# A hybrid SSD and gMLP step on one core: the opening's first weight tile reads the rows without the adaLN shift

## The chip, the cores and the metric

One core of one Trainium2 chip runs the whole kernel. The metric is the device time of one execution in microseconds (us), lower being better. The kernel before took a median of 1444.05 us over three runs, 1443.5 to 1444.36.

## The reference, cut to what matters

Two layers work on 640 rows of 1024 channels: 128 context rows (v = 0) and 512 latent rows (v = 1), each kind with its own conditioning vector `c`. What the change touches is the head of a layer:

```
mod = silu(c) @ w_ada + b_ada ; shift, scale, gate = split(mod, 3)
h = rms_norm(x, norm_w) * (1 + scale) + shift
proj = h @ w_in          # xbc, z, dt, u, v, z_g, gl_m, gl_g
```

`xbc` goes on into a depthwise convolution and a scan, `dt` into the decays of the scan, and the rest into two branches that are merged, projected and added to `x`. After two layers there is a final norm. Since the projection is linear, (s + shift) @ w = s @ w + shift @ w, where s is the scaled row without the shift; the second term is one column for the context rows and one for the latent rows.

## The kernel before, in words

Everything is kept transposed: channels on the 128 partitions, in eight chunks k = 0 to 7, and the 640 rows along the free axis. The weights come as tiles of 1024 by 128, numbered t; a layer has 88. For each tile SP loads half a megabyte into a slot of `w_st` (two slots), POOL splits it into a rounded high part `w_hi` and a rest `w_lo` in four quarters (lines 509 to 515), and PE multiplies it with the rows, which are split the same way. One chunk (line 600) is six matmuls of 320 columns: high weight with high row, low weight with high row, high weight with low row, two halves each. There are two accumulators, `acc[0]` and `acc[1]`.

The order of each engine's work is written out by hand, and semaphores tie the engines together. The opening of layer 0 is what this text is about:

- SP loads the conditioning vectors, the rows `xr`, small vectors, and then sixteen half-megabyte pieces of `w_ada`: four jobs of four pieces. A job (L, q, h) gives half h (channel chunks 0 to 3 or 4 to 7) of the scale (q = 1) or the shift (q = 0). The order before is scale half 0, shift half 0, scale half 1, shift half 1, by `JOBS_FIRST`. The narrow `dt` weight and tile 0 come after the eighth piece, tile 1 and six constants last.
- One job on PE is `first_mm` (line 670, two halves that each need two pieces), a `row_copy` on ACT (line 1026), `first_tp` on PE (line 681), and `job_out` on DVE (lines 1407 and 1412), which makes `mods` and, for a scale, the multiplier `amul`. `job_read` counts jobs that are out.
- `before(k)` on DVE (line 1473) makes `h_pre`, the row scaled but not shifted. `h_high(k)` on ACT (line 1045) adds the shift and rounds into `h_hi`. `h_low(k)` on DVE (line 1467) makes the rest `h_lo`, which lies in the place of `h_pre`.
- `dt` has a product of its own: DVE scales its narrow weight (`dt_scaled`, line 1452), PE multiplies the plain rows with it (`dt_part`, line 614) and adds the shift's part as two columns (`dt_shift`, line 622).
- `keep_pace` (line 656) are matmuls whose result nobody reads.
- `opening` runs chunks 0 to 3 of tile 0, with jobs 2 and 3 between and behind them, then `dt`, then chunks 4 to 7. After it, tile 1 and all others follow. POOL begins to split tile 2 when tile 0 is done (`tile_done`), and ACT moves tile 0's accumulator into `raw` (line 1180), from which DVE runs the convolution (lines 1618 and 1620).

Of the kernel before, what the change touches and what calls it, by code (L numbers as in the profile page):

```python
# [124 lines left out]
JOBS_FIRST = [(0, q, h) for h in (0, 1) for q in (1, 0)]  # L125
# [54 lines left out]
def build(nc, xT, wts, wada, cT, bada, normw, finalw, ssmw, convw, dtb, alog, dskip, lnw, lnb,  # L180
# [114 lines left out]
    bst = new("bst", [P, NCH, 12])  # L295
# [52 lines left out]
    dtrow_ready, raw_ready = sem("dtrow_ready"), sem("raw_ready")  # L348
    sel_ready, v_made = sem("sel_ready"), sem("v_made")
# [55 lines left out]
    def _(sp):  # L405
# [33 lines left out]
        for n in range(4 * NF):  # L439
            L, q, hf = JOBS_FIRST[n // 4]  # L440
            sp.dma_start(ada_first(n), wada[L, q, hf, n % 4, :, :, :]).then_inc(pre_in[n // 2], 16)
            if n == 7:
                dt_weight(0)
                weight(0, 0)
        weight(1, 1)
        load_consts()
# [36 lines left out]
    def _(pool):  # L483
# [32 lines left out]

        base = own.n
        for slot in range(2):
            split(slot, 16, None)
# [16 lines left out]
    def _(pe):  # L536
# [89 lines left out]
        def opening(hi, lo):  # L626

            ready = (hhi_ready, h_ready, 0)
            for k in range(KC // 2):
                chunk(0, k, hi, lo, ready)  # L630
                if k == 1:
                    first_mm(2)
            first_tp(2)
            first_mm(3)
            first_tp(3)
            dt_part(0, 1)
            pe.wait_ge(job_read, NF)
            dt_shift(0)
            for k in range(KC // 2, KC):
                last = chunk(0, k, hi, lo, ready)  # L640
            last.then_inc(tile_done, 1)
# [242 lines left out]
        first_mm(1, range(DTG))  # L884
        first_tp(0)
        keep_pace(2)
        first_mm(1, range(DTG, KC))
        keep_pace(2)
        first_tp(1)
        dt_part(0, 0)  # L890
        for L in range(DEPTH):
# [17 lines left out]
            if L == 0:  # L909
                opening(*h)  # L910
# [7 lines left out]
            for p in range(1, T_G):  # L918
# [5 lines left out]
                if p in V_AT:  # L924
                    v_tile(T0 + p, V_AT.index(p) % 2, hooks=hooks,
                           ready=(hhi_ready, h_ready, L) if L > 0 and p < RAWT + 2 else None)
                else:
# [30 lines left out]
    def _(act):  # L958
# [77 lines left out]
        row_copy(1)  # L1036

        for L in range(DEPTH):
# [23 lines left out]
            if L == 0:  # L1062
                act.wait_ge(job_read, 2)
                for k in range(KC // 2):
                    h_high(k)
                act.wait_ge(norm_in, 48)
                A(ea[:, :], ea[:, :], ACT.Exp).then_inc(ea_ready, 1)
                row_copy(2)
                row_copy(3)
                act.wait_ge(job_read, NF)  # L1070
                for k in range(KC // 2, KC):
                    h_high(k)
# [4 lines left out]
                free(("dt", 0), A(halves(c_buf[0]), a[:, :, 0:HALF], ACT.Copy))  # L1077
                evacuated(act, ("dt", 0))
# [71 lines left out]
            for p in range(T_UZ):  # L1150
# [28 lines left out]
                for dst, src in pieces(acc_of(t), *raw_row(i), L):  # L1179
                    last = A(dst, src, ACT.Copy)  # L1180
# [180 lines left out]
    def _(dve):  # L1361
# [93 lines left out]
        for L in range(DEPTH):  # L1455
# [39 lines left out]
            if L == 0:  # L1495
                dve.wait_ge(rbc_ready, 1)
                for half in range(2):
                    k0 = KC // 2 * half
                    if half == 1:
                        dve.wait_ge(ea_ready, 1)  # L1500
                        for d in range(DEPTH):
                            last = TS(ea_diag[:, d, :], ident[0:32, 0:32], ea[:, d:d + 1], None, ALU.mult)
                        last.then_inc(diag_ready, 1)
                        job_out(2)
                    before(k0)
                    before(k0 + 1)
                    dt_scaled(0, k0, k0 + KC // 2)
                    before(k0 + 2)
                    job_out(2 * half + 1)
                    before(k0 + 3)  # L1510
                    for k in range(k0, k0 + KC // 2):
                        h_low(k)
# [507 lines left out]
```

## Time and profile before

| what | us |
|---|---|
| median of three runs | 1444.05 |
| the profiled execution's own time | 1443.57 |
| its span | 1441.8 |
| PE busy | 1425.8 (99% of the span) |
| POOL busy | 1023.6 (71%) |
| DVE busy | 975.0 (68%) |
| ACT busy | 474.2 (33%) |

The profiled execution lies 0.48 us below the median and has 1.8 us around its span. Starts in the timelines are counted from the span's start. A timeline line merges instructions that follow each other: its second number runs from the first one's start to the last one's end, and the x number is their count. Matmuls overlap, so the pace of a group is read from the start of one line to the start of the next. "PEclk" is the granted clock of TensorE: 1.00 is 2.4 GHz and 0.50 is 1.2 GHz.

### The profile page before, as it was taken

The page shows a single profiled execution, that of the slowest core. Times are in us where ns is not written, and L with a number is a line of the kernel's source. Part 1 is how long each engine was busy: PE and PEld are TensorE (multiplying, and loading weights), DVE is VectorE, ACT ScalarE, POOL GpSimd, SP SyncE. Part 2 cuts the span into 40 slices and gives each one's busy share as a digit, 9 for nine tenths or more (in the row PEclk, how much of TensorE's full clock was granted, in tenths as well). Part 3 has the DMA queues.
Part 4 walks back from the last instruction along what each step waited for, and adds up shares of the span by engine and source line. Part 5 has one row for each costly group of instructions (what it writes and reads, how often), then busy time and mean ns, then how long its engine had stood idle before and what let it go on. Part 6 is the DMA issues. An engine that isn't in the chain of part 4 may idle for free.

```text
span 1441.8 us, 27057 instructions
## 1 busy us (share of the span) xinstructions
PE 1425.8 (99%) x10191; PEld 1388.0 (96%) x10191; DVE 975.0 (68%) x1454; ACT 474.2 (33%) x1086; POOL 1023.6 (71%) x1421
## 2 busy tenths in 40 slices
PE   8999999999999999999999999999999999999997
PEld 5999998999999999999999999989999999999997
DVE  5865576674767678988879676567566876867234
ACT  4331223313766333001243323241257661320122
POOL 2688875596555589998859897658765556979772
PEclk9999999999999999999999999999999999999999
DMA  9112333113565565444332232421346565453222
GB/s 358 60 64 78 129 106 121 63 62 116 152 193 183 158 253 194 152 151 138 115 132 74 78 122 93 134 63 59 103 127 181 170 189 186 161 187 118 74 74 88
DMA packets 113838, 189.54 MB, mean 131 GB/s; under 512 B 12736, under 2 KB 76352, under 8 KB 112320
## 3 DMA queue, kind: packets, MB, share of 16 engines
q1 hardware_dynamic: 42736, 138.34, 29.1%
q10 hardware_dynamic: 70992, 49.63, 11.5%
q8 instruction: 81, 1.33, 0.4%
q14 instruction: 29, 0.24, 0.0%
HBM read 169.79 MB, written 18.15 MB: 130 GB/s over the span
## 4 chain that ended last, share of the span: by engine, by line
PE 96%; DVE 2%; DMA 1%; SPq 0%; ACT 0%; issue 0%; DVEq 0%; ACTq 0%
PE acc L600 78%; PE acc L567 6%; PE X L840 2%; PE X L805 2%; PE X L567 1%; PE X L825 1%; PE X L872 1%; DMA ada_pre<-in_wada 1%; PE X L851 1%; PE X L759 1%; DVE cv L1620 1%; PE X L649 0%; PE acc L718 0%; DVE h_pre L1473 0%; DVE xr L1936 0%; PE X L812 0%
## 5 line engine op out<-in xcount | busy, mean ns | idle before, releaser
L510 POOL CAST w_hi<-w_st 128x256 fp32r<-128x256 f32 x704 | 419.8, 610 | 396.1 <-issue 182.6
L514 POOL TENSOR_TENSOR w_lo<-w_st,w_hi 128x256 fp32r<-128x256 f32 x704 | 641.5, 921 | 0.0
L600 PE MATMUL acc<-h_hi,w_hi 128*128 128x320 f32 x1744 | 406.3, 314 | 0.7 <-ACT h_hi L1045 0.7
L600 PE MATMUL acc<-h_lo,w_hi 128*128 128x320 f32 x1744 | 397.8, 309 | 1.1 <-DVE h_lo L1467 1.1
L600 PE MATMUL acc<-h_hi,w_lo 128*128 128x320 f32 x1744 | 397.2, 309 | 0.0
L600 PEld LDWEIGHTS acc<-h_hi,w_hi 128*128 128x128 f32 x1744 | 288.6, 188 | 10.5 <-issue 7.8
L600 PEld LDWEIGHTS acc<-h_lo,w_hi 128*128 128x128 f32 x1744 | 291.3, 188 | 1.8 <-DVE h_lo L1467 1.7
L600 PEld LDWEIGHTS acc<-h_hi,w_lo 128*128 128x128 f32 x1744 | 291.7, 188 | 0.0
L1620 DVE SCALAR_TENSOR_TENSOR cv<-raw,convw_sb,cv 128x642 f32<-128x642 f32 x128 | 134.9, 1054 | 4.5
L1387 DVE SCALAR_TENSOR_TENSOR ada_acc<-ada_st,sc,ada_acc 128x512 f32<-128x512 f32 x112 | 104.2, 969 | 1.8
L1141 ACT ACTIVATE cvt<-cv 128x642 f32<-128x642 f32 x32 | 23.8, 743 | 158.4 <-DVE cv L1620 158.4
L567 PE MATMUL acc<-w_hi,h_hi 128*128 128x256 f32 x256 | 73.2, 286 | 0.0
L567 PE MATMUL acc<-w_hi,h_lo 128*128 128x256 f32 x256 | 72.5, 283 | 0.0
L567 PE MATMUL acc<-w_lo,h_hi 128*128 128x256 f32 x256 | 72.4, 283 | 0.0
L1606 DVE TENSOR_TENSOR xw<-x_tok,ex 128x256 f32<-128x256 f32 x80 | 45.6, 613 | 37.7 <-PE X L805 37.4
L1724 DVE SCALAR_TENSOR_TENSOR gdt<-gm,tm,gdt 128x128 f32<-128x128 f32 x160 | 68.3, 485 | 1.1 <-ACT gdt L1279 0.8
L1618 DVE TENSOR_SCALAR cv<-raw,convw_sb 128x642 f32<-128x642 f32 x32 | 26.0, 811 | 63.0 <-ACT raw L1180 63.0
L1269 ACT ACTIVATE dmat<-cum_bc,ncf 128x128 f32<-128x128 f32 x160 | 62.5, 391 | 14.9 <-issue 14.1
L1310 ACT ACTIVATE c_buf<-acc 128x640 f32<-128x640 f32 x16 | 11.3, 705 | 159.1 <-PE acc L600 159.1
L1271 ACT ACTIVATE cum_bc<-cum_bc,ebs 128x128 f32<-128x128 f32 x160 | 62.1, 388 | 0.0
L600 PE MATMUL acc<-yg_hi,w_hi 128*128 128x320 f32 x256 | 60.2, 316 | 0.0
L1279 ACT ACTIVATE gdt<-gm,tm 128x128 f32<-128x128 f32 x160 | 51.1, 390 | 23.3 <-DVE gm L1735 16.6
(257 smaller groups left out, 2474.8 us busy)
## 6 DMA issues: line engine op xcount, KB each, us to landing
w_st<-in_wts SPq DMA_DIRECT2D x176, 512.0 KB, 3.6
cum_bc<-cum_dram ACTq DMA_DIRECT2D x80, 256.0 KB, 4.9
ada_st<-in_wada SPq DMA_DIRECT2D x33, 512.0 KB, 4.3
ex_bc<-ex_dram ACTq DMA_DIRECT2D x64, 128.0 KB, 3.2
ada_pre<-in_wada SPq DMA_DIRECT2D x15, 512.0 KB, 9.7
mga_dram<-c_buf SPq DMA_DIRECT2D x16, 320.0 KB, 6.0
xf<-xf_dram SPq DMA_DIRECT2D x4, 1280.0 KB, 7.7
mga<-mga_dram SPq DMA_DIRECT2D x2, 2560.0 KB, 10.0
```

The source lines that it names most:

```text
L510: nc.gpsimd.tensor_copy(quarter(w_hi, slot, q), quarter(w_st, slot, q)).then_inc(s_pool, 1)
L514: nc.gpsimd.tensor_tensor(quarter(w_lo, slot, q), quarter(w_st, slot, q), f(quarter(w_hi, slot, q)), ALU.subtract).then_inc(w_split, 1)
L567: last = mm(out.rearrange("p (t n) -> p t n", t=2), x[:, k, P * c:P * (c + 1)], w[:, s, :].rearrange("p (t k n) -> p k t n", t=2, n=P)[:, ...
L600: last = mm(a[:, hf, 0:n1], w[:, s, cols], x[:, k, hf * HALF:hf * HALF + n1], start=(k == 0 and n == 0), stop=(k == KC - 1 and n == 2))
L805: mm(X[3][:, cols], bt[:, s, :], xw[:, s, :, :, :].rearrange("p d h w -> p (d h w)")[:, cols], start=True, stop=True).then_inc(s_mm, 1)
L1269: last = A(dmat[:, n % 2, h, :], cum_bc[n % 2][:, 0, h, :], ACT.Identity, bias=ncf[:, c, j:j + 1])
L1271: last = A(cum_bc[n % 2][:, 1, h, :], cum_bc[n % 2][:, 1, h, :], ACT.Identity, bias=ebs[:, c, j:j + 1])
L1279: last = A(gdt[:, n % 2, h, :], gm[:, n % 2, 1, :], ACT.Copy, scale=tm[:, c, j:j + 1])
L1387: STT(out=o, in0=w, scalar=s, in1=o, op0=ALU.mult, op1=ALU.add)
L1606: last = TT(xw[:, a % 2, d, :, :], xg, per_head(ex[:, d, c, HPG * g:HPG * (g + 1)], HD), ALU.mult)
L1620: ins = STT(out=o, in0=r[:, tap:tap + CW], scalar=w[:, tap:tap + 1], in1=o, op0=ALU.mult, op1=ALU.add)
L1724: last = STT(out=gdt[:, s, h, :], in0=gm[:, s, 0, :], scalar=tm[:, c, j:j + 1], in1=gdt[:, s, h, :], op0=ALU.mult, op1=ALU.add)
```

## The change

The jobs are reordered: scale half 0, scale half 1, shift half 0, shift half 1. The loads go: four pieces of `w_ada`, the `dt` weight, tile 0, the six constants, ten pieces, tile 1, two pieces. Tile 0 is multiplied with the unshifted rows: ACT rounds `h_pre` into `p_hi` (`scaled_high`), DVE writes the rest into `h_hi`'s place (`scaled_low`), and `first_chunk` uses the two. The shift's halves are split into `sh_hi` and `sh_lo`, two columns for each chunk, and `first_shift` adds 24 two-column matmuls to the same accumulator, 12 for each half. ACT then adds those two columns as a bias when it moves tile 0 into `raw`. `h_hi` and `h_lo` with the shift are still made as before, now for tile 1 on, in whose chunks PE waits for them one by one. The scaling of the `dt` weight moves from DVE to POOL, between the splits of tiles 0 and 1. `sh_hi` and `sh_lo` share the place of a small buffer of the gMLP statistics, and `p_hi` is the buffer that layer 1's first tiles use already.

```diff
-JOBS_FIRST = [(0, q, h) for h in (0, 1) for q in (1, 0)]
+JOBS_FIRST = [(0, q, h) for q in (1, 0) for h in (0, 1)]
...
         for n in range(4 * NF):
...
-            if n == 7:
+            if n == 3:
...
-        weight(1, 1)
-        load_consts()
+                load_consts()
+            if n == 13:
+                weight(1, 1)
...
+        def dt_scaled(half):
+            k = slice(KC // 2 * half, KC // 2 * (half + 1))
+            if half == 0:
+                pool.wait_ge(dtw_in, 16)
+            pool.wait_ge(amul_ready, half + 1)
+            for v in range(2):
+                last = nc.gpsimd.tensor_tensor(dts[:, k, v, :], dtw[:, k, :],
+                                               amul[:, 0, v, k].unsqueeze(2).broadcast_to([P, KC // 2, 32]), ALU.mult)
+            last.then_inc(dts_ready, 1)
         base = own.n
         for slot in range(2):
+            if slot == 1:
+                dt_scaled(0)
+                dt_scaled(1)
             split(slot, 16, None)
             split_hi(slot, 0)
...
-        def opening(hi, lo):
-            ready = (hhi_ready, h_ready, 0)
-            for k in range(KC // 2):
-                chunk(0, k, hi, lo, ready)
-                if k == 1:
-                    first_mm(2)
+        def first_chunk(k):
+            a, cols = acc_of(0), slice(k * P, (k + 1) * P)
+            if k == 0:
+                pe.wait_ge(row_out, 1)
+            split_in(0, k)
+            for n, (w, x) in enumerate(((w_hi, p_hi), (w_lo, p_hi), (w_hi, h_hi))):
+                pe.wait_ge(qlo_ready if n == 2 else qhi_ready, k + 1)
+                for hf in range(2):
+                    last = mm(a[:, hf, 0:HALF], w[:, 0, cols], x[:, k, hf * HALF:(hf + 1) * HALF],
+                              start=(k == 0 and n == 0), stop=(k == KC - 1 and n == 2 and hf == 0))
+            if k % 4 == 3:
+                last.then_inc(q_used, 1)
+        def first_shift(half):
+            a = acc_of(0)
+            pe.wait_ge(shhi_ready, half + 1)
+            pe.wait_ge(shlo_ready, half + 1)
+            for k in range(KC // 2 * half, KC // 2 * (half + 1)):
+                for n, (w, x) in enumerate(((w_hi, sh_hi), (w_lo, sh_hi), (w_hi, sh_lo))):
+                    last = mm(a[:, 1, HALF:HALF + 2], w[:, 0, k * P:(k + 1) * P], x[:, k, :],
+                              start=False, stop=(k == KC - 1 and n == 2))
+            if half == 1:
+                last.then_inc(tile_done, 1)
+        def opening():
+            first_mm(1, range(DTG))
+            first_chunk(0)
+            first_mm(1, range(DTG, KC))
+            first_chunk(1)
+            first_tp(1)
+            first_chunk(2)
+            first_mm(2, range(DTG))
+            first_chunk(3)
+            dt_part(0, 0)
+            first_mm(2, range(DTG, KC))
+            first_chunk(4)
             first_tp(2)
-            first_mm(3)
+            first_chunk(5)
+            first_mm(3, range(DTG))
+            first_chunk(6)
+            dt_part(0, 1)
+            first_chunk(7)
+            first_mm(3, range(DTG, KC))
+            first_shift(0)
             first_tp(3)
-            dt_part(0, 1)
             pe.wait_ge(job_read, NF)
             dt_shift(0)
-            for k in range(KC // 2, KC):
-                last = chunk(0, k, hi, lo, ready)
-            last.then_inc(tile_done, 1)
+            first_shift(1)
...
         first_mm(0, range(DTG, KC))
         keep_pace(2)
         stat_bc(0)
-        first_mm(1, range(DTG))
+        keep_pace(1)
         first_tp(0)
-        keep_pace(2)
-        first_mm(1, range(DTG, KC))
-        keep_pace(2)
-        first_tp(1)
-        dt_part(0, 0)
+        keep_pace(4)
...
+                elif L == 0 and p == 1:
+                    tile(T0 + p, *h, hooks=hooks, ready=(hhi_ready, h_ready, 0), ks=range(KC))
...
-        row_copy(1)
...
         for L in range(DEPTH):
...
             if L == 0:
-                act.wait_ge(job_read, 2)
-                for k in range(KC // 2):
-                    h_high(k)
+                def scaled_high(k):
+                    act.wait_ge(hpre_ready, k + 1)
+                    A(p_hi[:, k, 0:TOK], h_pre[:, k, :], ACT.Copy).then_inc(qhi_ready, 1)
+                def shift_high(half):
+                    act.wait_ge(job_read, 3 + half)
+                    k = slice(KC // 2 * half, KC // 2 * (half + 1))
+                    A(sh_hi[:, k, :], mods[:, 0, :, k].rearrange("p v k -> p k v"), ACT.Copy).then_inc(shhi_ready, 1)
+                for k in range(3):
+                    scaled_high(k)
+                row_copy(1)
+                scaled_high(3)
                 act.wait_ge(norm_in, 48)
...
+                scaled_high(4)
                 row_copy(2)
+                for k in range(5, KC):
+                    scaled_high(k)
+                shift_high(0)
+                act.wait_ge(q_used, 1)
+                h_high(0)
+                h_high(1)
...
-                act.wait_ge(job_read, NF)
-                for k in range(KC // 2, KC):
-                    h_high(k)
+                h_high(2)
+                h_high(3)
+                shift_high(1)
                 act.wait_ge(consts_in, 16 * 6)
                 act.wait_ge(dt_done, 1)
...
                 own.link(A(bsh[:, RAWT, :], a[:, 1, HALF:HALF + 2], ACT.Identity, bias=dtb_sb[:, 0:1]))
                 free(("dt", 0), A(halves(c_buf[0]), a[:, :, 0:HALF], ACT.Copy))
+                act.wait_ge(q_used, 2)
+                for k in range(KC // 2, KC):
+                    h_high(k)
                 evacuated(act, ("dt", 0))
...
-                for dst, src in pieces(acc_of(t), *raw_row(i), L):
-                    last = A(dst, src, ACT.Copy)
+                if t == 0:
+                    own.link(A(bsh[:, 0, :], acc_of(t)[:, 1, HALF:HALF + 2], ACT.Copy))
+                for n, (dst, src) in enumerate(pieces(acc_of(t), *raw_row(i), L)):
+                    last = A(dst, src, ACT.Identity, bias=bsh[:, 0, min(n, 1):min(n, 1) + 1]) if t == 0 else \
+                        A(dst, src, ACT.Copy)
                 free(t, last)
...
             if L == 0:
+                def scaled_low(k):
+                    dve.wait_ge(qhi_ready, k + 1)
+                    TT(h_hi[:, k, :], h_pre[:, k, :], f(p_hi[:, k, 0:TOK]), ALU.subtract).then_inc(qlo_ready, 1)
+                def shift_low(half):
+                    dve.wait_ge(shhi_ready, half + 1)
+                    k = slice(KC // 2 * half, KC // 2 * (half + 1))
+                    TT(sh_lo[:, k, :], mods[:, 0, :, k].rearrange("p v k -> p k v"), f(sh_hi[:, k, :]), ALU.subtract)\
+                        .then_inc(shlo_ready, 1)
...
-                for half in range(2):
-                    k0 = KC // 2 * half
-                    if half == 1:
-                        dve.wait_ge(ea_ready, 1)
-                        for d in range(DEPTH):
-                            last = TS(ea_diag[:, d, :], ident[0:32, 0:32], ea[:, d:d + 1], None, ALU.mult)
-                        last.then_inc(diag_ready, 1)
-                        job_out(2)
-                    before(k0)
-                    before(k0 + 1)
-                    dt_scaled(0, k0, k0 + KC // 2)
-                    before(k0 + 2)
-                    job_out(2 * half + 1)
-                    before(k0 + 3)
-                    for k in range(k0, k0 + KC // 2):
-                        h_low(k)
+                before(0)
+                before(1)
+                scaled_low(0)
+                before(2)
+                scaled_low(1)
+                before(3)
+                scaled_low(2)
+                job_out(1)
+                before(4)
+                scaled_low(3)
+                before(5)
+                scaled_low(4)
+                before(6)
+                scaled_low(5)
+                job_out(2)
+                before(7)
+                scaled_low(6)
+                shift_low(0)
+                scaled_low(7)
+                dve.wait_ge(ea_ready, 1)
+                for d in range(DEPTH):
+                    last = TS(ea_diag[:, d, :], ident[0:32, 0:32], ea[:, d:d + 1], None, ALU.mult)
+                last.then_inc(diag_ready, 1)
+                dve.wait_ge(qlo_ready, KC)
+                h_low(0)
+                job_out(3)
+                for k in range(1, 4):
+                    h_low(k)
+                shift_low(1)
+                for k in range(4, KC):
+                    h_low(k)
                 dve.wait_ge(consts_in, 16 * 6)
                 own.link(TS(convw_sb[:, :, :, :], convw_sb[:, :, :, :], 0.5, None, ALU.mult))
...
```

## Rows read from the trace of the kernel before

**Rows 1.** The page: the span, the engines, the chain that ended last.
```profile
span 1441.8 us, 27057 instructions
PE 1425.8 (99%) x10191; PEld 1388.0 (96%) x10191; DVE 975.0 (68%) x1454; ACT 474.2 (33%) x1086; POOL 1023.6 (71%) x1421
PE 96%; DVE 2%; DMA 1%; SPq 0%; ACT 0%; issue 0%; DVEq 0%; ACTq 0%
```

**Rows 2.** Waits of PE from 43.3 us on: for what, total us, times, longest.
```profile
PE X L735 <- ACT c_buf L1328: 1.4, 1, 1.4
PE X L743 <- DVE rst L1930: 0.8, 1, 0.8
```

**Rows 3.** Timeline of PE: start, length, line, shapes, [idle before, releaser].
```profile
16.05 1.06 PE L670 MATMUL acc<-ada_pre,scp 128*32 128x512 f32 x8 [0.18 <-DMA ada_pre<-in_wada]
...
18.65 1.06 PE L670 MATMUL acc<-ada_pre,scp 128*32 128x512 f32 x8
19.64 1.05 PE L681 MATMUL X<-sel,ada_row 128*128 128x2 f32 x8
20.56 1.11 PE L656 MATMUL acc<-tri,ident 128*128 128x256 f32 x4
21.60 1.06 PE L670 MATMUL acc<-ada_pre,scp 128*32 128x512 f32 x8
...
31.23 0.56 PE L600 MATMUL acc<-h_hi,w_hi 128*128 128x320 f32 x2
...
32.21 0.46 PE L600 MATMUL acc<-h_hi,w_hi 128*128 128x320 f32 x2
...
33.10 0.95 PE L681 MATMUL X<-sel,ada_row 128*128 128x2 f32 x8
...
37.60 1.29 PE L614 MATMUL acc<-xr,dts 128*32 128x128 f32 x24
38.70 0.28 PE L622 MATMUL acc<-mods,dtw 128*32 128x2 f32 x16
39.24 0.53 PE L600 MATMUL acc<-h_hi,w_hi 128*128 128x320 f32 x2 [0.25 <-ACT h_hi L1045]
...
43.41 0.45 PE L600 MATMUL acc<-h_hi,w_hi 128*128 128x320 f32 x2
```

**Rows 4.** Timeline of DVE.
```profile
8.51 6.02 DVE L1421 TENSOR_TENSOR ssq<-ssq,c_buf 128x640 f32<-128x640 f32 x7 [0.21 <-ACT c_buf L1006]
...
34.08 0.17 DVE L1407 TENSOR_TENSOR mods<-X,bada_sb 128x8 f32<-128x8 f32 x1 [3.11 <-PE X L681]
...
34.48 1.92 DVE L1473 SCALAR_TENSOR_TENSOR h_pre<-xr,amul,X 128x128 f32<-128x128 f32 x4
...
39.13 3.82 DVE L1467 SCALAR_TENSOR_TENSOR h_lo<-h_pre,mods,h_hi 128x128 fp32r<-128x128 f32 x8
```

**Rows 5.** Timeline of ACT.
```profile
35.97 0.60 ACT L1026 ACTIVATE ada_row<-X 128x512 f32<-128x512 f32 x1 [4.00 <-PE X L670]
38.08 3.74 ACT L1045 ACTIVATE h_hi<-h_pre,mods 128x128 fp32r<-128x128 f32 x8 [1.52 <-DVE mods L1407]
...
41.99 0.71 ACT L1077 ACTIVATE c_buf<-acc 128x640 f32<-128x640 f32 x1
```

**Rows 6.** Timeline of POOL.
```profile
23.03 0.80 POOL L510 CAST w_hi<-w_st 128x256 fp32r<-128x256 f32 x2 [20.35 <-DMA w_st<-in_wts]
...
25.89 1.47 POOL L514 TENSOR_TENSOR w_lo<-w_st,w_hi 128x256 fp32r<-128x256 f32 x2
```

**Rows 7.** Windows: busy us of PE, PEld, DVE, ACT, POOL, then PEclk, DMA, GB/s.
```profile
35.30:39.20 3.90, 2.97 (x56) 1.93 (x48) 3.82 (x11) 1.72 (x4) 3.90 (x8) 1.00 0.06 21
1431.50:1434.50 3.00, 0.83 (x7) 0.69 (x6) 2.29 (x6) 1.22 (x3) 0.00 (x0) 1.00 0.64 231
1434.50:1435.00 0.50, 0.27 (x2) 0.03 (x1) 0.50 (x2) 0.00 (x0) 0.00 (x0) 0.73 1.02 378
1435.00:1438.00 3.00, 0.00 (x0) 0.00 (x0) 3.00 (x6) 0.00 (x0) 0.00 (x0) 0.50 0.77 273
```

More of the change, by code:

```diff
@@ L294, in build @@
     lnw_sb = new("lnw_sb", [P, DEPTH, KC])
-    bst = new("bst", [P, NCH, 12])
+    r_b = region(4 * 12 * NCH)
+    bst = place("bst", [P, NCH, 12], r_b)
+    sh_hi, sh_lo = place("sh_hi", [P, KC, 2], r_b, F32R), place("sh_lo", [P, KC, 2], r_b + 8 * KC, F32R)
     mv = new("mv", [P, NCH, 2])
@@ L348, in build @@
     dtrow_ready, raw_ready = sem("dtrow_ready"), sem("raw_ready")
+    qhi_ready, qlo_ready, q_used = sem("qhi_ready"), sem("qlo_ready"), sem("q_used")
+    shhi_ready, shlo_ready = sem("shhi_ready"), sem("shlo_ready")
     sel_ready, v_made = sem("sel_ready"), sem("v_made")
@@ L909, in _ @@
             if L == 0:
-                opening(*h)
+                opening()
             else:
```

## The prediction

> **What bounds the kernel now.** I read the page's shares and the chain first. PE is busy for 1425.8 of 1441.8 us and is 96% of the chain that ended last [rows 1]: the kernel takes what PE takes, plus the moments in which PE stands still. Then I listed PE's waits from 43.3 us on. The two longest are 1.4 and 0.8 us, and both lie in the last ten microseconds [rows 2]; between the opening and the tail PE waits for almost nothing. So whatever this change does, it does to one number: the moment at which tile 1 begins. That is 43.41 us, the last line of [rows 3]. Everything after it is a rigid block that moves with it. The question is then what PE must do before tile 1, and for whom it waits there, and for that I read the timelines of the opening engine by engine [rows 3 to 6].
>
> **PE's queue in the opening, new order.** The prices are paces, from one start to the next, in [rows 3]. Half a `first_mm` takes 0.99 us (18.65 to 19.64), a `first_tp` 0.92 (19.64 to 20.56), two `keep_pace` 1.04 (20.56 to 21.60), so one 0.52. A chunk that follows another kind of work takes 0.98 (31.23 to 32.21), and in the new order every chunk does. Half a `dt_part` takes 1.10 (37.60 to 38.70), `dt_shift` 0.28.
> The two-column matmuls of `first_shift` are not in the trace. They load 128 by 128 weights and stream two columns, and the nearest row in both is `first_tp`: 8 records in 0.92 us, 0.115 each. Twelve of them make 1.38 us for a half, 2.76 for both. From below they are bounded by `dt_shift`, 16 records in 0.28 us with 32-column weights, 0.018 each, so 0.4 for all 24. From above, by a chunk's six matmuls in 0.98, 0.16 each, so 3.9 for all. The Trainium skill, "TensorE: Matmul & The Clock Gate", section "Wait — 56ns, not 53.3ns?", gives about 25 ns as the least from one small matmul to the next; by that alone all 24 would be 0.6 us and the sum 2.2 us smaller. The rows of `first_tp` speak against it, since their weight load (128 columns) is not hidden under so short a stream.
>
> Now the sum. `first_tp(0)` starts 0.47 us sooner than before: after 18.65 there is one `keep_pace` (0.52) where half a `first_mm` (0.99) was, so at 19.17. From there to the start of `first_tp(3)` PE has: `first_tp(0)` 0.92, four `keep_pace` 2.08, six halves of `first_mm` 5.94, eight chunks 7.84, `first_tp(1)` and `(2)` 1.84, two halves of `dt_part` 2.20, `first_shift(0)` 1.38. That is 22.20, so `first_tp(3)` starts at 41.37, if PE never waits on the way.
>
> Does it wait? By DMA: the transfers keep their total. Between 16.05 us, where PE had waited for pieces 2 and 3 [rows 3], and 23.03, when POOL gets tile 0 [rows 6], four pieces, tile 0 and 0.13 MB of `dt` weight came, 2.75 MB in 6.98 us, so 1.33 us for half a megabyte. In the new order tile 0 is in at about 17.7, pieces 4 and 5 at 20.7, then every pair 2.65 us later (23.4, 26.0, 28.7, 31.4), tile 1 at 32.7, the last pair at 35.4. PE asks for them at 22.2, 24.2, 28.1, 31.2, 35.1 and 39: never late, by 0.8 us at the least. SP waits for no semaphore until tile 2, so the earlier constants hold up only the pieces behind them, which is in these times (0.13 MB, 0.3 us). By POOL: a split is 4.3 us from 23.03, so tile 0 is split by 22.1, its first quarter at 19.3; the two dt scalings that follow (four operations on 128 elements, 0.2 to 0.9 each by the cast and the subtraction on 256 in [rows 6]) end before 29 and are asked for at 30 and 37. Behind them stands the split of tile 1, which starts with its landing at 32.7. By DVE: one `before` costs 0.92 to 0.96 (its two instructions twice in 1.92 [rows 4]), `scaled_low`, a subtraction on 640 elements, 0.78 (the seven sums over 640 take 6.02, 0.86 each with their waits [rows 4]). With `job_out(1)` after `first_tp(1)` and `job_out(2)` after `first_tp(2)` at about 33, the low part of chunk 7 is there at 37.3, and PE asks for it at 38.7. By ACT: a copy of 640 elements is 0.71 to 0.74 [rows 5]; `row_copy(2)` now stands ahead of `scaled_high(5)`, which so comes at 33.5 for a chunk that wants it at 33.9. The thinnest place, but it holds. I charge no wait here, and up to 1 us if DVE is slowed while POOL splits tile 1 beside it.
>
> **The end of the opening.** Here the new order is a chain and not a queue. `first_tp(3)` starts at 41.37. DVE's `job_out(3)` begins 0.98 us after the start of a `first_tp` (33.10 to 34.08 [rows 3, 4]) and takes 0.17: 42.5. `h_low(1)`, `(2)`, `(3)` stand behind it on DVE and ahead of `shift_low(1)`: 3.82 us for four [rows 4], so 0.955 each, 2.87, until 45.4. `shift_low(1)` is one small operation, 0.17: 45.6. Only then can `first_shift(1)` run, 1.38, and tile 1 begins at 47.0. PE meanwhile does `dt_shift` (0.28, to 42.8) and then stands still for 2.8 us. DVE had itself stood still before `job_out(3)`, since `h_low(0)` ends near 38.7, but `h_low(1)` is put behind the job.
>
> Against 43.41 this is +3.6 us. Said as a balance: from `first_tp(0)` at 19.64 to 43.41 the old order had 20.6 us of work by the same paces (four `first_tp` 3.68, four `keep_pace` 2.08, five halves of `first_mm` 4.95, chunks 7.4, `dt` 2.48) and so 3.2 of waits. These go, and `first_tp(0)` comes 0.47 sooner. Against them stand 2.76 us of two-column matmuls, 3.1 of waiting for `job_out(3)` and `shift_low(1)`, half a `first_mm` that has moved behind `first_tp(0)` (0.99), and 0.4 because chunks no longer follow each other: 7.2 less 3.7 is 3.6 with the rounding. Tile 0's chunks were never what the loads held up for long, so there is little to win by freeing them.
>
> **What follows tile 1.** Its chunks wait for `h_low` one by one. `h_low(4)` ends at 46.5 and `(7)` at 49.4, PE wants them at 50.5 and later: free. ACT's `h_high(4)` to `(7)` come after `dt`'s copy (0.24 and 0.71 [rows 5]) at 43.9 to 47.6, ahead of DVE. Tile 0's move to `raw` costs one small ACT operation more (0.24), and DVE is free for the convolution only at 49.6, 2.6 us behind the start of tile 1, where it was 1.1. No PE wait from there to the tail was longer than a few tenths [rows 2], and PE's own queue hides this 1.5; if it did not, it would cost up to that. Splits by POOL and loads by SP hang on `tile_done`, and move with the block.
>
> **Sum.** The profiled execution took 1443.57 us, so with the change 1447.2. That execution lies 0.48 below the median of 1444.05; the median with the change is then 1447.65, and I say 1447.7.
>
> **Rivals.**
> *The clock falls in the wait.* In [rows 7] PEclk goes from 1.00 (2.4 GHz) to 0.50 (1.2 GHz) in the tail, at about 1434.75, after 3 us in which PE was busy for 0.83. From 35.3 to 39.2 PE was busy for 2.97 of 3.90 and kept 2.4 GHz. The new opening has, from 40 us on, 1.4 us of two-column matmuls, 0.9 of `first_tp`, 0.3 of `dt_shift`, 2.8 of nothing and again 1.4 of two columns. That resembles the tail more than the old opening. If the clock falls there, the first matmuls of tile 1 run at 1.2 GHz, and each microsecond there does half a microsecond's work; for some 4 us, no row shows how long, +2 us: 1449.7. The same page of the Trainium skill, section "What's actually happening", says that recent activity sets the clock, which is on this rival's side. Chance 0.27.
> *PE's queue alone decides.* If `shift_low(1)` did not matter (DVE far ahead of my times, or `h_low` cheap), tile 1 would start at 41.37 + 0.92 + 0.2 + 0.28 + 1.38 = 44.2, +0.8: 1444.8. The order on DVE speaks against it, by three rows of 0.955. Chance 0.08.
> *Two-column matmuls at the lower bound.* 0.42 us for all in place of 2.76, with DVE's chain as above: +1.3, 1445.3. Chance 0.10. Together with the case before it gives the other side: cheap two-column matmuls and no wait, 44.2 less 2.3, so 41.9 and 1442.5, faster. It decides as soon as the 24 cost under about 0.05 each and `shift_low(1)` is out by the time that `dt_shift` ends. Chance 0.03.
> *DVE and POOL in each other's way.* `scaled_low(5)` to `(7)` fall on the split of tile 1, or the convolution's 1.5 us is not hidden: +1 to +1.5, 1448.7 to 1449.2. Chance 0.12.
> The forecast itself has 0.40, with its own range 1446.7 to 1448.6 from the paces.
>
> **How the numbers follow.** A change below 0.2% (2.9 us, about what a measurement of this kernel can tell) counts as none; the line is at 1446.95. The forecast is above it in most of its range (0.34 of 0.40), the clock and DVE rivals wholly (0.39), the two low ones are below. Slower 0.73, the same 0.24, faster 0.03. The range leaves out the ends: 1445.0 to 1450.4.
>
> **What would show it.** In the new profile: PE's first L600 line of tile 1 near 47.0; a PE wait of 2.5 to 3 us for DVE's `sh_lo` just before it, and hardly any between 20 and 41; two groups of 12 two-column matmuls of about 1.4 us; on DVE three `h_low` between the last `mods` and the second `sh_lo`; a PEclk of 1.00 in the windows from 42 to 52, or 0.5 in part of them if the first rival is right. The prediction is wrong if PE reaches `first_tp(3)` much before 41, if the second `sh_lo` is ready by 43, or if PE's waits after tile 1 grow by more than a few tenths.

## The result and the profile after

The changed kernel took 1451.05 us (median of 5 runs, 1450.05 to 1452.23), the kernel before 1444.05. The ratio is 1.0047, with an interval of 1.0036 to 1.0058: slower, by 7.0 us where 3.6 was forecast, and 0.65 us above the upper end of the range. The profiled execution took 1450.86 us, with a span 7.3 us longer than before. Shares of the page of the changed kernel, as in [rows 1]:

```profile
span 1449.1 us, 27144 instructions
PE 1433.0 (99%) x10217; PEld 1394.4 (96%) x10217; DVE 983.3 (68%) x1460; ACT 481.9 (33%) x1097; POOL 1028.8 (71%) x1425
PE 97%; DVE 2%; DMA 0%; ACT 0%; issue 0%; DVEq 0%; SPq 0%; ACTq 0%
```

PE is busy for 7.2 us more, and the chain is PE's in the same share. Where the time lies is told by PE's waits in the changed kernel (total us, times, longest), against [rows 2]:

```profile
PE acc L666 <- DVE sh_lo L1578: 2.7, 1, 2.7
PE X L790 <- ACT c_buf L1403: 1.4, 1, 1.4
PE X L798 <- DVE rst L2030: 0.8, 1, 0.8
...
PE acc L641 <- DVE mods L1482: 0.3, 1, 0.3
```

The two waits of the tail are the same to a tenth. The wait for `sh_lo` is new. PE's timeline at the end of the opening, after (start, length, line, shapes, [idle before, releaser]), answers to [rows 3]:

```profile
19.01 0.95 PE L736 MATMUL X<-sel,ada_row 128*128 128x2 f32 x8
...
40.22 0.27 PE L666 MATMUL acc<-sh_hi,w_hi 128*128 128x2 f32 x1
...
41.58 1.03 PE L736 MATMUL X<-sel,ada_row 128*128 128x2 f32 x8
42.88 0.33 PE L641 MATMUL acc<-mods,dtw 128*32 128x2 f32 x16 [0.26 <-DVE mods L1482]
45.94 0.34 PE L666 MATMUL acc<-sh_hi,w_hi 128*128 128x2 f32 x1 [2.73 <-DVE sh_lo L1578]
46.15 0.35 PE L666 MATMUL acc<-sh_hi,w_lo 128*128 128x2 f32 x1
...
48.50 0.88 PE L619 MATMUL acc<-h_hi,w_hi 128*128 128x320 f32 x2
...
53.37 0.47 PE L619 MATMUL acc<-h_hi,w_hi 128*128 128x320 f32 x2
```

And DVE beside it, after, against [rows 4]:

```profile
42.66 0.17 DVE L1482 TENSOR_TENSOR mods<-X,bada_sb 128x8 f32<-128x8 f32 x1 [3.63 <-PE X L736]
42.86 2.86 DVE L1542 SCALAR_TENSOR_TENSOR h_lo<-h_pre,mods,h_hi 128x128 fp32r<-128x128 f32 x6
45.64 0.16 DVE L1578 TENSOR_TENSOR sh_lo<-mods,sh_hi 128x8 fp32r<-128x8 f32 x1
45.72 3.78 DVE L1542 SCALAR_TENSOR_TENSOR h_lo<-h_pre,mods,h_hi 128x128 fp32r<-128x128 f32 x8
```

This is the chain that was forecast, step for step. DVE idles for 3.63 us before the job's output, with `h_low(1)` to `(3)` queued behind it, and then PE idles while DVE does them. What differs is the clock. Windows of the changed kernel (busy us of PE, PEld, DVE, ACT, POOL, then PEclk, DMA, GB/s):

```profile
40.00:43.00 3.00, 2.74 (x38) 2.43 (x36) 0.31 (x2) 2.55 (x6) 0.31 (x1) 1.00 0.42 153
...
43.00:44.00 1.00, 0.21 (x16) 0.12 (x12) 1.00 (x3) 0.71 (x3) 0.00 (x0) 0.51 0.18 66
...
43.00:53.00 10.00, 7.27 (x45) 7.21 (x42) 9.48 (x20) 5.93 (x15) 4.19 (x5) 0.50 0.02 7
53.00:54.00 1.00, 1.00 (x8) 1.00 (x7) 1.00 (x1) 0.00 (x0) 1.00 (x2) 0.87 0.00 0
```

The granted clock is 1.2 GHz from 43.0 to 53.3 us. It was down 0.2 us before the wait for `sh_lo` began: `dt_shift` (42.88 and 0.33 long) ended at 43.21, and the window from 43.00 to 44.00 has it at 0.51 with PE still busy for its first 0.21 us. The twelve two-column matmuls of `first_shift(1)` take from 45.94 to 48.50, 0.213 each, where those of `first_shift(0)` at 2.4 GHz took 0.113 (40.22 to 41.58). Tile 1 then has 18 matmuls from 48.50 to 53.37, 4.87 us. In the kernel before, the same 18 end at this row of PE's timeline, 2.63 us after 43.41:

```profile
46.04 0.46 PE L600 MATMUL acc<-h_hi,w_hi 128*128 128x320 f32 x2
```

So the 7.3 us are: 3.6 forecast and found; 1.2 for twelve small matmuls at 1.2 GHz (2.56 less 1.36); 2.2 for the start of tile 1 (4.87 less 2.63); 0.3 of small differences. The clock's part is 3.4 us; the 2.7 us of the wait passed at 1.2 GHz too, but cost nothing by that.

### The profile page after: what moved, and what is told of

It reads as the page before. It is cut to its first block, busy times and chain, and to the rows that moved or that the text cites. A ratio compares the mean times of both kernels' runs of the same rounds, so it can differ in the third digit from the quotient of the medians.

```text
span 1449.1 us, 27144 instructions
## 1 busy us (share of the span) xinstructions
PE 1433.0 (99%) x10217; PEld 1394.4 (96%) x10217; DVE 983.3 (68%) x1460; ACT 481.9 (33%) x1097; POOL 1028.8 (71%) x1425
## 4 chain that ended last, share of the span: by engine, by line
PE 97%; DVE 2%; DMA 0%; ACT 0%; issue 0%; DVEq 0%; SPq 0%; ACTq 0%
PE acc L619 77%; PE acc L586 6%; PE X L895 2%; PE X L860 2%; PE X L586 1%; PE X L880 1%; PE X L927 1%; PE X L906 1%; PE X L814 1%; PE acc L654 1%; DVE cv L1720 1%; PE X L704 0%; PE acc L773 0%; DMA xr<-in_xT 0%; DVE ssq L1496 0%; DVE xr L2036 0%
```

## The experiments

Each median is against the kernel before on the same chip: 1444.37 us beside e1 to e4, 1443.81 beside e5 to e8, 1443.76 beside e9, e10, e12 and e14. A trace shows one execution, and where that one lay far from the median the text says so. Two theories: the clock falls because of the wait for `sh_lo` (then filling or removing the wait brings it back), or it falls because of what the end of the opening is made of (then removing the wait isn't enough).

### e1_filled_wait: full matmuls in the wait

```
             dt_shift(0)
+            for _ in range(5):
+                mm(X[2][:, 0:2 * P], ident[:, :], tri[:, :, :].rearrange("p d n -> p (d n)"), start=True, stop=True)
             first_shift(1)
```

> Five keep-pace matmuls into a free bank stand between dt_shift and first_shift(1), in the 2.7 us that PE waits there; nothing else changes, and they should end before the wait does (5 x 0.52 = 2.6 us). Theory: the clock falls because PE stands still in that wait, and that is 3.4 of the 7 us lost (12 two-column matmuls at 0.213 in place of 0.112, 1.2 us, and 18 matmuls of tile 1 at 0.267 in place of 0.147, 2.2 us). Then PEclk is 1.00 throughout, tile 1 starts at 47.3 in place of 48.5, and the time is 3.4 us below the changed kernel's, near 1447.5. Rival: the two-column matmuls and the small ones before them are what brings the clock down; then it falls all the same and the time stays at 1450 to 1451.

1447.96 us (1447.16 to 1451.74, 6 runs), ratio 1.0031 [1.0018, 1.0043]: 3.1 us faster than the changed kernel, with five matmuls more. Its timeline of PE, and its windows:

```profile
43.41 2.43 PE L697 MATMUL X<-tri,ident 128*128 128x256 f32 x10
...
47.57 0.53 PE L619 MATMUL acc<-h_hi,w_hi 128*128 128x320 f32 x2
```

```profile
44.00:46.00 2.00, 1.84 (x9) 1.28 (x7) 2.00 (x6) 2.00 (x5) 0.00 (x0) 1.00 0.02 4
46.00:48.00 2.00, 1.76 (x15) 1.79 (x16) 2.00 (x7) 2.00 (x5) 0.12 (x1) 1.00 0.00 0
```

The clock stays at 1.00 in this trace, and the kernel is 3.6 us over the one before. That equals the forecast to a tenth, with some luck: in the trace tile 1 starts 4.2 us later than before (47.57 for 43.41), and the span is 4.2 us longer. The two parts of the loss are thus separated, to half a microsecond: 3.6 to 4.2 for the longer opening, 3.1 to 3.4 for the clock. One of the six runs took 1451.74 us at a mean granted clock of 0.994, like the changed kernel's runs (0.994 and 0.995), where the other five had 0.996 to 0.998. So the filling does not hold the clock in every run.

### e2_shift_low_first: the wait taken away

```
                 job_out(3)
-                for k in range(1, 4):
-                    h_low(k)
                 shift_low(1)
-                for k in range(4, KC):
+                for k in range(1, KC):
                     h_low(k)
```
ACT's `shift_high(1)` stands ahead of `h_high(2)` too.

> shift_low(1) on DVE and shift_high(1) on ACT stand right behind the last job instead of behind h_low(1) to (3) and h_high(2), (3). Theory: the wait of 2.7 us at first_shift(1) is only the order on DVE; PE starts first_shift(1) at about 43.3, tile 1 at 44.7, the clock does not fall, and the time is 1.3 us above the kernel before: 1444.9 to 1445.4. Rival 1: the clock falls without the wait, then tile 1 pays at least 2 us more: 1447 to 1448. Rival 2: h_low(1) to (3) are then late for tile 1, whose chunks 1 and 2 want them at 45.6 and 46.5 when they end at 44.2, 45.1, 46.0: nothing, or some tenths.

A miss: 1449.76 us (1448.98 to 1453.36), 1.0045 [1.0032, 1.0059]. `first_shift(1)` started at 43.41 and tile 1 at 45.96, 2.5 us sooner than in the changed kernel, but by the medians only 1.3 us of it was left. Its windows, and a wait of PE that is new:

```profile
42.00:44.00 2.00, 1.53 (x24) 1.39 (x25) 1.08 (x4) 1.22 (x4) 0.00 (x0) 0.68 0.63 241
44.00:46.00 2.00, 2.00 (x11) 2.00 (x11) 2.00 (x5) 1.97 (x6) 0.00 (x0) 0.50 0.00 0
```

```profile
PE X L835 <- DVE tm L1663: 1.4, 1, 1.4
```

PE idled for only 0.5 us, and the clock fell at about 42.7 (a mean of 0.68 between 1.00 and 0.50). Then the convolution, which ends in `tm`, was late by 1.4. It came back at 49.5, after 6.8 us, where it had been down for 10.2 in the changed kernel. The wait for `sh_lo` was therefore not needed for the fall, as the changed kernel's own trace says too. What e1 and e2 fit is that the long wait prolongs the stretch at 1.2 GHz, but with one trace of each that is not shown.

### e3_lows_ahead: four `h_low` in DVE's own idle time

```
-                h_low(0)
-                job_out(3)
-                for k in range(1, 4):
+                for k in range(4):
                     h_low(k)
+                job_out(3)
                 shift_low(1)
```
ACT's `row_copy(3)` stands behind `h_high(3)`.

> As the version with shift_low(1) first, and h_low(1) to (3) and h_high(2), (3) stand ahead of the last job, in the 3.6 us in which DVE stood idle before it. Theory: PE's queue alone decides, so tile 1 starts at 44.7 as there and the time is the same to 0.3 us, 1444.9 to 1445.4, though DVE is free for the convolution at 46.9 instead of 49.6. Rival: the late convolution costs PE something later; then this one is about 1 us faster than the version with shift_low(1) first alone.

A miss: 1448.19 us (1447.68 to 1450.02), 1.0027 [1.0017, 1.0037]. The profiled run is the slowest of the nine, 1.8 us above the median, so its trace isn't that of the typical run. In it the wait for `sh_lo` went to 0.3, but PE had waited 2.0 us for adaLN pieces early on, so `first_tp(3)` came at 43.58; the clock fell at 47.0, and `tm` was waited for 1.2. DVE's `h_low(4)` to `(7)` show a further price, in its timeline:

```profile
47.23 6.21 DVE L1542 SCALAR_TENSOR_TENSOR h_lo<-h_pre,mods,h_hi 128x128 fp32r<-128x128 f32 x8 [1.91 <-ACT h_hi L1097]
```

In the changed kernel the same eight took 3.78 us (45.72), with POOL idle until 48.81. Here they fall on POOL's split of tile 2, from 47.11. The Trainium skill, "GPSIMD Engine Reference", section "1. Specifications", says that VectorE instructions with two SBUF inputs contend with GpSimd; `h_pre` and `h_hi` are two, and this trace agrees. It is not always DVE that is slowed: in e1 the eight took 3.78 us, and the first two casts of POOL's split beside them (from 47.88) took 2.99 us, for 0.80 in e3.

### e4_one_column_pair: e3 without the small matmuls

The loop of `first_shift` keeps its last matmul alone, so 23 of 24 are left out (and with them most of the shift's product for tile 0).

> As the version with the lows ahead, with 23 of the 24 two-column matmuls left out (so the first tile's shift is incomplete); waits stay. Theory: each is 0.112 to 0.115 us of PE's queue and all of it is on the path: 2.6 us less than the version with the lows ahead, 1442.3 to 1442.8, below the kernel before. Rival: they are issued in the shadow of a wait for job_out(3) and shift_low(1); then only the second half's 12 count, 1.3 us less, 1443.6 to 1444.1.

A miss: 1447.48 us (1447.13 to 1450.07), 1.0024 [1.0013, 1.0034]. Tile 1 began at 44.44, but without the small matmuls PE waited 0.9, 0.6, 0.3 and 0.6 us in their place, and `tm` was waited for 1.2. Its windows:

```profile
40.00:42.00 2.00, 1.08 (x11) 0.68 (x7) 2.00 (x5) 0.60 (x2) 0.17 (x1) 1.00 0.15 35
42.00:44.00 2.00, 0.92 (x21) 0.69 (x20) 1.06 (x4) 0.79 (x3) 0.03 (x1) 1.00 0.59 227
44.00:46.00 2.00, 1.56 (x6) 1.56 (x7) 0.68 (x2) 2.00 (x5) 2.00 (x5) 0.55 0.01 4
```

No price of a small matmul can be read from it. It shows that the clock falls without those 23 too, where short waits leave PE busy for 2.00 of 4.00 us and `first_tp(3)` and `dt_shift` are most of what it does.

### e5_chunk_between and e6_cums_later: PE's order spread, the convolution given time

e5 is e3 with `first_shift(0)` and `first_tp(3)` ahead of chunk 7. e6 is e5 with one line of the tile loop changed:

```
-                if p == (2, 6)[L]:
+                if p == (3, 6)[L]:
                     dt_cums2(L)
```

> As the version with the lows ahead, but PE's order is chunk 6, dt_part, first_mm(3) second half, first_shift(0), first_tp(3), chunk 7, dt_shift, first_shift(1): six full matmuls of 320 columns now stand in the middle of the small ones, over the waits for the last row copy and the last job. Theory: the clock fell in the two versions before because three and more microseconds in a row hold nothing but two-column matmuls and short gaps; with the chunk between, PEclk stays 1.00, tile 1 starts at 44.1 to 44.5, and what is left is 0.9 us there and the 1.2 us that PE later waits for tm: 1445.5 to 1446.3. Rival: the clock falls all the same (the chunk is only 0.9 us), then 1447.5 to 1448.5.

> As the version with chunk 7 between, with PE's cumulative sums of dt (dt_cums2) moved behind tile 3 instead of tile 2. Theory: the new wait of 1.2 us for DVE's tm comes from h_low(4) to (7) being slow and late beside POOL's split of tile 2, and one tile of 7.2 us is room enough: the wait is gone, 1.2 us less than the version without it. Rival: the lateness of the convolution surfaces at another place, such as the accumulator of tile 2 that ACT must free: no gain.

e5: 1448.12 us (1447.8 to 1449.09), 1.0030 [1.0018, 1.0041]. e6: 1448.37 (1447.85 to 1448.9), 1.0031 [1.0020, 1.0042]. Both miss. The clock fell at 42.3 in e5 and 43.9 in e6, although no wait there was over 0.5 us. The window of e5:

```profile
42.00:43.00 1.00, 0.53 (x9) 0.25 (x12) 0.86 (x3) 0.11 (x1) 0.00 (x0) 0.64 0.68 111
```

In e5 the wait for `tm` was absent already, so e6 had nothing to remove: its convolution began 4.9 us behind the start of tile 1 (50.94 for 46.07), that of e3 6.9 (53.65 for 46.80).

### e8_before_with_small and e14_before_with_full: the kernel before, with each kind of matmul

The cleanest pair, on the kernel before; at the same place, behind `dt_shift(0)`, e8 adds

```
+            for k in range(24):
+                mm(X[2][:, 0:2], w_hi[:, 0, k % 4 * P:(k % 4 + 1) * P], h_hi[:, k % 4, 0:2], ...)
```

and e14, with no e8 in it,

```
+            for _ in range(5):
+                mm(X[2][:, 0:2 * P], ident[:, :], tri[:, :, :].rearrange("p d n -> p (d n)"), start=True, stop=True)
```

> The kernel before, with 24 two-column matmuls (results unused, into a free bank) behind dt_shift and ahead of chunk 4. Theory: each costs 0.112 us of PE's queue, 2.7 us in all; they follow a stretch of low work from 35 to 39 us, so the clock falls as in the changed kernel and adds 1.5 to 2.5 us more: 1447.8 to 1449. Rival 1: the clock does not depend on them: +2.7 us less the 0.5 us of waits for h_high(4) and h_low(4) that they cover, 1446.2. Rival 2: they are covered by DVE's chain of h_low: no change.

> The control for the kernel before with 24 small matmuls: in their place stand five keep-pace matmuls of 256 columns, whose pace elsewhere is 0.52 us each, so 2.6 us in place of 2.7, results unused. Theory: it is not the time spent but how little the array does in it that brings the clock down; PEclk stays 1.00, and the cost is 2.6 us less the 0.5 us of waits that they cover: 1445.9 to 1446.4. Rival: the extra time alone, or the place, brings the clock down: 1448.3 to 1449.5 as with the small ones.

e8: 1449.08 us (1448.28 to 1449.56, 5 runs), 1.0035 [1.0021, 1.0049], +5.3. e14: 1444.93 (1444.63 to 1446.23, 11 runs), 1.0007 [0.9998, 1.0017], +1.2, less than expected. PE's timeline and the windows of e8:

```profile
36.11 1.05 PE L683 MATMUL X<-sel,ada_row 128*128 128x2 f32 x8 [0.72 <-ACT ada_row L1028]
37.09 1.29 PE L614 MATMUL acc<-xr,dts 128*32 128x128 f32 x24
38.20 0.28 PE L622 MATMUL acc<-mods,dtw 128*32 128x2 f32 x16
38.41 4.74 PE L640 MATMUL X<-h_hi,w_hi 128*128 128x2 f32 x24
43.01 0.88 PE L600 MATMUL acc<-h_hi,w_hi 128*128 128x320 f32 x2
```

```profile
38.00:40.00 2.00, 2.00 (x34) 1.84 (x27) 1.96 (x4) 2.00 (x6) 1.50 (x3) 0.76 0.00 0
40.00:42.00 2.00, 2.00 (x11) 2.00 (x11) 2.00 (x5) 1.97 (x6) 0.00 (x0) 0.50 0.54 191
44.00:46.00 2.00, 2.00 (x10) 2.00 (x10) 0.00 (x0) 0.00 (x0) 0.00 (x0) 0.53 0.00 0
```

The same of e14:

```profile
38.79 2.43 PE L640 MATMUL X<-tri,ident 128*128 128x256 f32 x10
40.87 0.64 PE L600 MATMUL acc<-h_hi,w_hi 128*128 128x320 f32 x2
```

```profile
38.00:40.00 2.00, 2.00 (x38) 1.54 (x29) 1.93 (x5) 1.92 (x5) 1.36 (x2) 1.00 0.03 8
40.00:42.00 2.00, 2.00 (x13) 1.87 (x12) 2.00 (x6) 1.97 (x6) 0.00 (x0) 1.00 0.64 194
```

In e8 PE has no gap from 36.11 on, and is busy for 2.00 of 2.00 us in each of these windows. The clock falls all the same, at about 39.0 (a mean of 0.76 over 38 to 40), and stays down until 45.9. In e14, behind the same wait of 0.72 us and the same narrow work, it holds. The two kernels differ only in the matmuls put in, so two-column matmuls, which the profile counts as busy, bring the clock down where wide ones hold it. They are not shown to do it by themselves: only six of the 24 had started by 39.0, and `first_tp`, `dt_part` and `dt_shift` stood ahead of them. The Trainium skill, "TensorE: Matmul & The Clock Gate", section "What's actually happening", says that the clock follows how busy TensorE has been of late. The trace agrees only if busy isn't read from PE's busy time, which was full in e8 for the 2.9 us before the fall.
As a sum for e8: at 0.112 each 24 are 2.7 us, and [rows 3] had waits there that absorb some; the rest of the 5.3 is the clock. The 24 took 4.60 us (38.41 to 43.01).

### e12_filled_no_pairs: what the small matmuls cost with the clock held

e1 without 23 of the 24 (their product is left out, as in e4).

> The changed kernel with the filled wait, and 23 of the 24 two-column matmuls left out (so the first tile's shift is incomplete). With the clock held this prices them. Theory: 12 of them stand before first_tp(3), which comes 1.3 us sooner, and 11 behind the wait, another 1.3: 2.6 us less than the filled version, 1445.1 to 1445.7. Rival: the shorter opening makes PE wait for a row copy or a landing instead: 1 us of it comes back.

A miss: 1449.48 us (1447.42 to 1452.89, 6 runs), 1.0039 [1.0026, 1.0051]. The six fall into two groups, three at 1447.4 to 1447.9 and three at 1451.1 to 1452.9, so the median stands for neither, and even the lower group is no faster than e1. The trace is of the upper group (1451.06). In it tile 1 did start sooner, at 45.84 for 47.57. But then `h_low(4)` to `(7)` fell on POOL's split and took 5.32 us, the convolution was late, PE waited 2.4 us for it until 64.63, and the clock fell half a microsecond later, at 65.2. Wait and windows of PE:

```profile
PE X L836 <- DVE tm L1666: 2.4, 1, 2.4
```

```profile
60.00:64.00 4.00, 2.19 (x15) 1.93 (x14) 3.65 (x6) 2.56 (x3) 2.55 (x6) 1.00 0.46 129
64.00:68.00 4.00, 3.37 (x21) 2.47 (x22) 3.86 (x6) 0.00 (x0) 4.00 (x5) 0.64 0.01 2
```

The price of the small matmuls could be read only as far as tile 1: 1.7 us for 23, with 0.9 us of new waits in their place, 2.6 in all or about 0.11 each.

### e7, e9 and e10: the shift as fp32 in 32-column groups, with and without full matmuls

e7 is e6 with `first_shift` rewritten; `sh_hi` and `sh_lo`, their operations on ACT and DVE and the wait for them are gone:

```
-                for n, (w, x) in enumerate(((w_hi, sh_hi), (w_lo, sh_hi), (w_hi, sh_lo))):
-                    last = mm(a[:, 1, HALF:HALF + 2], w[:, 0, k * P:(k + 1) * P], x[:, k, :], ...)
+                for w in (w_hi, w_lo):
+                    for j in range(4):
+                        at = k * P + 32 * j
+                        last = mm(a[32 * j:32 * j + 32, 1, HALF:HALF + 2], f(w[:, 0, at:at + 32]),
+                                  mods[:, 0, :, k], ...)
```

e9 adds 256-column matmuls to e7: two behind `first_shift(0)`, one ahead of `dt_shift`, one ahead of tile 1. e10 adds three to e7 (one ahead of `dt_shift`, two ahead of tile 1), moves chunk 7 and `first_tp(3)` ahead of `first_shift(0)`, `row_copy(3)` ahead of `h_high(2)` and `job_out(3)` ahead of `h_low(2)`.

> As the version with the cumulative sums later, with first_shift done like dt_shift: plain fp32 matmuls with weights of 32 columns, four column groups at once, for w_hi and w_lo with the unsplit shift; sh_hi and sh_lo are not made. 128 records for both halves at 0.018 each, as dt_shift's 16 in 0.28 us, are 2.3 us in place of 2.7, and the 0.5 us in which PE waited for shift_high and shift_low go. Theory: 0.9 us less than the version before, which would be 1443.4 to 1444.2, level with the kernel before the change. Rival: the 32-column loads pass at twice that pace when they are 64 in a row, or the clock falls: 1 to 3 us more.

> As the version with the shift in column groups, with four keep-pace matmuls of 256 columns: two after first_shift(0), where PE waits 0.6 us for the row copy, one before dt_shift (0.5 us of waiting), one before tile 1 (0.45). Theory: they fall mostly into waits, cost 0.6 us at most and hold the clock at 1.00, which in that version cost 2.6 us or so in tile 1: 1444.6 to 1445.4. Rival: four are not enough, PEclk falls near 43 us again and the time is 1447 to 1448.

> As the version with the shift in column groups, with chunk 7 over the last row copy, first_shift(0) behind first_tp(3) over the last job, job_out(3) on DVE behind h_low(1) instead of h_low(3), and three keep-pace matmuls in what waits are left. Theory: first_tp(3) starts at 40.1, the last job is out at 41.3, dt_shift at 42.2, tile 1 at 43.4 to 43.8, and with the clock held the kernel takes 1443.6 to 1444.2, level with the kernel before. Rival 1: the clock falls, 1446.5 to 1447.5. Rival 2: the opening is shorter than I count and it wins: 1442.8 to 1443.5.

e7: 1447.04 us (1445.95 to 1449.35), 1.0024 [1.0014, 1.0034], a miss. e9: 1445.22 (1444.68 to 1446.2, 11 runs), 1.0009 [1.0000, 1.0018], as expected; its trace is of the slowest of the eleven. e10: 1444.69 (1444.19 to 1447.35, 11 runs), 1.0009 [1.0000, 1.0018], half a us above what was expected. Windows of e7, and of e9:

```profile
42.00:44.00 2.00, 1.40 (x83) 1.05 (x81) 0.82 (x3) 0.66 (x2) 0.00 (x0) 0.82 0.79 254
44.00:46.00 2.00, 1.64 (x6) 1.64 (x7) 0.69 (x2) 2.00 (x5) 1.92 (x5) 0.50 0.06 16
```

```profile
42.00:44.00 2.00, 2.00 (x88) 1.65 (x87) 0.86 (x3) 0.55 (x2) 0.00 (x0) 1.00 0.57 218
```

e7 shows that the small matmuls can be cheap: 64 records in some 0.75 us for a half (0.65 by the pace in e9), where twelve of 128 columns took 1.36. Tile 1 began at 44.36 in e7 and at 44.47 in e9, with four matmuls more. The clock fell at 43.3 in e7 and held in e9, and tile 1 took 7.96 us in e7 (44.36 to 52.32) and 5.38 in e9 (44.47 to 49.85), 2.6 less. By the medians e9 is 1.8 us faster; its own trace lost about 1 us after that point, a wait of 0.5 for POOL's `w_lo` among it. In e10 tile 1 began here:

```profile
43.62 0.65 PE L619 MATMUL acc<-h_hi,w_hi 128*128 128x320 f32 x2
```

That is 0.2 us behind the kernel before, with the clock held, and e10 is 6.4 us faster than the change as it was made. It is not faster than the kernel before; no version was.

## Why the prediction was off

**What held.** The step sizes of PE's queue: `first_tp(0)` at 19.01 (forecast 19.17), `first_tp(3)` at 41.58 (41.37), no wait worth naming between, the small matmul at 0.113 (0.115). The chain at the end: `mods` at 42.66 (42.5), three `h_low` in 2.86 (2.87), `sh_lo` done at 45.80 (45.6), PE idle for 2.73 (2.8). Some of this is luck: from `first_tp(0)` to `first_tp(3)` the eight chunks took 8.6 us for the 7.84 in the sum, and `first_tp` and `keep_pace` half a microsecond less than theirs. That DVE's order, and not the matmuls, set the last 2.7 us was shown by e2, where `first_shift(1)` started at 43.41. e1, which is this sum with the clock held, measured +3.6 by the medians and +4.2 in its trace, for +3.6.

**What failed** is the step that left TensorE's clock at 2.4 GHz through the end of the opening: the sum has no term for it. A fall there was named as the first rival, with 0.27 against the forecast's 0.40, and it is what happened, though not "in the wait": the clock was down at 43.0, and the wait began at 43.21. Within that rival a term was too small as well: "some 4 us" at the low clock, +2. The rows show 10.2 us low, of which PE stood still for 2.7 from 43.21 on; the rest cost 1.2 in `first_shift(1)`, which the rival had not priced at all, and 2.2 in tile 1. The clock came back only 4.8 us into tile 1's back-to-back matmuls. With 3.4 in place of 2 the rival gives 1451.1, which is what was measured; that it is the same to a tenth is luck, since the trace has 0.3 us more of small differences.

**Why the chance was too low.** The argument for it leaned on the wait, and set the stretch 35.3 to 39.2 of [rows 7] against it, where PE was busy for 2.97 of 3.90 us and kept the clock. But busy time counts two columns behind a 128-column weight load like 512 columns. What had changed was the mix: in the old opening each `first_tp` stood between full matmuls, in the new one twelve small matmuls of `first_shift(0)`, eight of `first_tp(3)` and the sixteen narrow ones of `dt_shift` came together, with only 0.26 us of waiting among them, and then the long wait. e8 shows that the mix is enough. In the changed kernel's trace the mix came first as well, since the clock fell 0.2 us before the long wait. That the wait counts too is shown by e1, where filling it kept five of six runs fast. How the two share the 3.4 us is open: e2, without the wait, still had its clock down for 6.8 us.

**The other rivals.** PE's queue alone (0.08) is the case that e2 made. Its tile 1 started at 45.96 and not at 44.2: 1.2 us of that is the clock, the rest is that `first_shift(1)` came at 43.41 and not at 42.8. Cheap two-column matmuls (0.10) were refuted by 0.113, and e7 shows the form in which they would be cheap. Their lower bound was read too high: 0.018 was the length of `dt_shift`, 0.28 us, over its sixteen, and by the pace in e9 (42.98 to 43.13) it is 0.009 each. DVE and POOL in each other's way (0.12) was absent from the changed kernel, whose long wait put `h_low(4)` to `(7)` ahead of POOL's split. It appeared once the opening was shorter (e2, e3, e4, e12), and the convolution's 1.5 us, said to be hidden, then cost 1.2 to 2.4.

**Where the expected gain of the experiments went.** Six of them (e2 to e7) shortened the opening and expected 1442.3 to 1446.3, and e12 1445.1 to 1445.7. Each mechanism took the time back in turn: the clock (e2 to e7), `tm` (e2, e3, e4, e12). How much of e3 is the early wait for pieces, which was 2.0 us in its profile and 0.2 to 0.9 in e5, e6 and e10, isn't settled; each has one profile.

## What to carry to other kernels

When work is reordered, look at what kind of matmuls come to lie together, and not only at how long PE is busy. Small matmuls bunched together brought the clock down here, with a wait behind them or without, and this doubled the loss. A few 256-column matmuls in the wait held it in five of six runs, 3.1 us for no useful work. An operation of 0.16 us queued behind three long ones that don't need to be first cost PE the whole of those three, 2.7 us. Before a stretch is shortened, ask what was hidden under it.

## What the hardware showed that was not expected

- The granted clock fell with PE's records at 2.00 of 2.00 us busy (e8), and with 0.5 us idle (e2). In the changed kernel it fell 0.2 us before PE's long wait, and in e12 half a microsecond after one.
- Matmuls of 128 by 128 weights and two columns pace at 0.112 us at 2.4 GHz and 0.213 us at 1.2 GHz; plain fp32 ones with 32-column weights at about 0.010 (64 records in 0.65 us, e9), like the sixteen of `dt_shift` (0.15 us, e9).
- Five 256-column matmuls in sequence took 2.08 us (e14), 0.42 each, where 0.52 had been read from pairs.
- Eight `h_low` operations took 3.78 us with POOL idle for most of them and 6.21 us beside its split (e3). In e1 they took 3.78 us beside the split, and POOL's two casts 2.99 us for 0.80.
